# Moving the first head's operand preparation into the projection block of a two-layer encoder step, with key stores ahead of value stores and sink sums by column

## The chip, the cores and the metric

The kernel runs on one core of one Trainium2 chip. The metric is the device time of one execution in microseconds (us), lower is better; for the kernel before, three runs are given by their median. The engines are PE (TensorE, matmul; PEld are its weight loads), DVE (VectorE), ACT (ScalarE), POOL (GpSimd) and SP (SyncE, which here only issues DMAs and waits).

## The reference

One inference step of an encoder trunk of two layers over 1024 prompt rows and 32 sample rows, model width 1024, all in float32. Each layer projects the normalised rows to queries, keys, values and forget gates, runs three groups of attention heads of width 64, normalises each group, projects back, and runs a squared-ReLU MLP; each half ends in a residual sum and a layer norm. The three groups differ in their reach and bias:

```
A: 6 heads, 2 key/value heads   own chunk of 64 + 2 before, T5 bias, a learned sink per head
B: 5 heads                      own chunk + 8 before, clipped relative bias
C: 5 heads                      causal over all rows, logit += sum of log forget gates
...
s = q . k * d ** -0.5 + bias
m = max(max_s(s), sink)                                   (A; the others have no sink)
p = exp(s - m);  p = p / (sum_s(p) + exp(sink - m))
o = p . v
```

The new keys and values of the prompt and of the sample are outputs as well, as are the logs of the forget gates.

## The kernel before, in words

**Blocks.** The program is a sequence of blocks, per layer: the in-projection, prompt attention, sample attention, out-projection, MLP. In a block every engine has its own list of instructions, executed in order, and the engines wait for each other by semaphores written out by hand. A block ends in a barrier of all engines, so the next one begins when the last engine is through.

**In-projection (from line 986).** The weights come as ten chunks, `IN_CH`: three of keys (0 to 2), three of values (3 to 5), four of queries (6 to 9). Each is loaded by SP into one of two buffers `w_raw`, split into a high and a low part (ACT writes the high part, `high_part`, L1162; POOL subtracts, `low_parts`, L1058, and then frees the buffer through `raw_free`), and used by PE in three passes (L378, L1117). Keys and queries are projected transposed into `qk_t`, read by DVE (L1207, L1209); values go row-wise into `v_rows` (L1245). During the value chunks PE turns the keys of each tile of 128 rows back (`turn_k`, L1095, two halves per tile), DVE copies them into the one buffer `k_stage` (L1253), and SP stores them to the outputs (`store_k`, L1007). DVE may write the next tile's keys only when the stores of the tile before have landed (L1250). Between these, DVE works off ten condition tiles (`conditions`, L292): each is a 128x1024 tile of adaLN weights, loaded by SP (`sp_conditions`, L283) into one buffer as soon as DVE has released it. In SP's list the load of the last of these tiles (number 9) stands ahead of the weights of chunk 7, of the value stores and of the last three key stores (L1040 to L1046). At the end DVE reads query tile 7, finishes the cumulated gates, and SP stores them for use as the bias of the C heads.

**Prompt attention (from line 1328).** The 16 heads are worked off in the order A, B, C, each in eight items: one item is 128 query rows, from the last to the first. Per item PE computes the scores from stacked operands (`scores`, L1440: keys in a high and a low part, each twice, over 128 partitions; queries stacked as high and low part), DVE adds the bias and takes the row maximum (`logits`, L1564), ACT takes the exponential and its row sum (L1506), PE turns the probabilities (L1456), ACT and DVE split them into two parts (L1519, L1572), PE multiplies by the values (L1472), and DVE adds the two halves (`head_out`, L1582). After a head's last item DVE forms the inverse of the row sums (L1593); for an A head it first adds the exponentials of the sinks, one operation on 128x8 (L1589). POOL prepares the operands ahead: key parts for each new key head (L1390 to L1395), query parts (L1402, L1404), the mask in the corners of the bias tile (L1408, L1409), value parts (L1416, L1418), and it scales the finished heads (L1381). Keys, queries, bias and values have two buffers each, by the number of the head.

**The start of prompt attention.** For the first head ACT copies the first key head into both halves of `keys_hi` (L1492) after it has loaded its tables, DVE subtracts (L1536), then makes `minus_sink` (L1538), the rounded identity (L1540) and the rounded causal mask (L1541, `causal_r`). POOL makes the first queries and, when SP's bias DMA (L1346) has landed, the masks. PE waits for the rounded constants, the keys and the queries:

```
                    pe.wait_ge(d_rounded, 2)
                    scores(0)
```

`raw` (the two `w_raw` buffers) lies at the start of the work area, `w_hi` and `w_lo` after it. In attention the queries and biases of both buffers lie where `w_raw` was, the key parts where `w_hi` was.

Of the kernel before, what the change touches and what calls it, by code (L numbers as in the profile page):

```python
# [17 lines left out]
F32 = mybir.dt.float32  # L18
# [5 lines left out]
P = 128  # L24
# [42 lines left out]
def build(nc, io):  # L67
# [28 lines left out]
    with ExitStack() as ctx:  # L96
# [96 lines left out]
        ks_hi = [at(f"keys_hi{s}", D0 + 4096 * s, [P, SEQ], F32R) for s in range(2)]  # L193
        ks_lo = [at(f"keys_lo{s}", D0 + 8192 + 4096 * s, [P, SEQ], F32R) for s in range(2)]
# [3 lines left out]
        q_st = [at(f"queries{s}", W0 + 4096 * s, [P, SEQ], F32R) for s in range(2)]  # L198
        bias_h = [at(f"bias{s}", W0 + 8192 + 4096 * s, [P, SEQ]) for s in range(2)]
# [365 lines left out]
        GROUPS = ((0, 384), (384, 320), (704, 320))  # L565

# [357 lines left out]
        for l in range(DEPTH):  # L924
# [60 lines left out]

            with nc.Block() as block:
                @block.sync
                def _(sp):
# [51 lines left out]
                    sp_conditions(sp, "B", l, 9, 10)  # L1040
                    sp_weights(sp, l, 7, 1)
                    for t in range(NTT):
                        sp.wait_ge(b_ev, V_EV - NTT + t + 1)
                        store("v", t, v_tok[:, t, :], b_vout)
                        if t % 3 == 2:
                            store_k(6 + t // 3)  # L1046
                    sp_weights(sp, l, 8, 2)
                    sp.wait_ge(b_rows, 3)
# [4 lines left out]
                def _(pool):  # L1053
# [24 lines left out]
                    for n in range(2, IN_CH):  # L1078
                        low_parts(n)
                        if n < 8:  # L1080
                            products(done, done + (4, 4, 3, 4, 4, 1)[n - 2])
                            done += (4, 4, 3, 4, 4, 1)[n - 2]

# [57 lines left out]
                def _(act):  # L1141
# [46 lines left out]
                    high_part(9)  # L1188

                @block.vector  # L1190
                def _(dve):
# [107 lines left out]
                    query(6)  # L1299
                    query(7)  # L1300
# [14 lines left out]
            span = {"a": 2, "b": 5, "c": NPT}  # L1315
# [12 lines left out]
            with nc.Block() as block:  # L1328
                @block.sync
                def _(sp):  # L1330
                    def bias(hn):
                        g, h = heads[hn][0:2]
                        if hn >= 2:
                            sp.wait_ge(d_lg, NPT * (hn - 1))
                        if g == "a":
                            dst, src = bias_h[hn % 2][:, 0:2 * P], bass.AP(scr_a.tensor, h * P * EXT_A + 127,
                                                                           [[EXT_A - 1, P], [1, 2 * P]])
                        elif g == "b":
                            dst, src = bias_h[hn % 2][:, 0:5 * P], bass.AP(scr_b.tensor, (l * BH + h) * (P * EXT_B) + 127,
                                                                           [[EXT_B - 1, P], [1, 5 * P]])  # L1340
                        else:
                            if h == 0:
                                sp.wait_ge(b_fout, 32)
                            dst, src = bias_h[hn % 2][:].rearrange("p (i t) -> p i t", t=P), \
                                bass.AP(scr_f.tensor, h * P, [[0, P], [CH * P, NPT], [1, P]])
                        sp.dma_start(dst, src).then_inc(d_bias[hn % 2], 16)  # L1346

                    sp.wait_ge(b_bias, 16 * (BH + (AH if l == 0 else 0)))
                    bias(0)
# [19 lines left out]
                def _(pool):  # L1369
# [13 lines left out]
                    for hn, (g, h, qt, half, kt, vc, oc) in enumerate(heads):  # L1383
# [16 lines left out]
                        q = qk[a:a + 64, qt, 0:SEQ]  # L1400
                        hi = q_st[s][a:a + 64, :]
                        own.did(pool.tensor_copy(hi, q))  # L1402
                        own.settle()
                        own.did(pool.tensor_tensor(q_st[s][64 - a:128 - a, :], q, hi.bitcast(F32), ALU.subtract), d_qb)  # L1404
                        if g != "c":
                            w = span[g] * P
                            pool.wait_ge(d_bias[s], 16 * (hn // 2 + 1))
                            own.did(pool.memset(bias_h[s][0:64, w - 64:w], -MASKED), d_mask)  # L1408
                            own.did(pool.memset(bias_h[s][64:P, 0:64], -MASKED), d_mask)  # L1409
                        if first_of[m] == hn:  # L1410
# [4 lines left out]
                            own.settle()  # L1415
# [10 lines left out]
                def _(pe):  # L1426
                    def scores(n):
# [3 lines left out]
                        if i == NPT - 1:  # L1431
                            pe.wait_ge(*((d_kb, m) if m else (d_first, 2)))
                            pe.wait_ge(d_qb, hn + 1)
                        if n >= 2:
                            pe.wait_ge(d_lg, n - 1)
# [40 lines left out]
                    pe.wait_ge(d_rounded, 2)  # L1476
# [10 lines left out]
                def _(act):  # L1487
                    load_tables(act)
                    first = heads[0]
                    a0 = 64 * first[3]  # L1490
                    for a in (a0, 64 - a0):
                        act.activation(ks_hi[0][a:a + 64, :], qk[a0:a0 + 64, Q_TILES + first[4], 0:SEQ], ACT.Copy)\  # L1492
                            .then_inc(d_first_hi, 1)
# [36 lines left out]
                def _(dve):  # L1530
                    own = Own(dve, dve_step)
                    first = heads[0]
                    a0 = 64 * first[3]
                    for i, a in enumerate((a0, 64 - a0)):
                        dve.wait_ge(d_first_hi, i + 1)
                        dve.tensor_tensor(ks_lo[0][a:a + 64, :], qk[a0:a0 + 64, Q_TILES + first[4], 0:SEQ],  # L1536
                                          ks_hi[0][a0:a0 + 64, :].bitcast(F32), ALU.subtract).then_inc(d_first, 1)
# [38 lines left out]
                    def head_out(n):  # L1576
# [7 lines left out]
                        if i == 0:  # L1584
                            c = slice(NPT * (hn % 2), NPT * (hn % 2 + 1))
                            dve.wait_ge(d_ex, n + 1)
                            if heads[hn][0] == "a":
                                dve.wait_ge(d_es, hn + 1)
                                own.did(dve.tensor_tensor(den[:, c], den[:, c], esk[:, c], ALU.add))  # L1589
# [720 lines left out]
```

## Time and profile before

| | us |
|---|---|
| median of three runs | 3181.93 |
| lowest, highest | 3179.59, 3183.39 |
| the profiled execution | 3183.84 |
| span of the profiled execution, first to last instruction | 3182.1 |
| PE busy in the span | 2924.9 (92%) |
| DVE busy | 1581.2 (50%) |
| POOL busy | 1525.1 (48%) |
| ACT busy | 875.0 (27%) |

The span is the stretch the trace covers; what lies around it is 1.7 us. A busy share says how long an engine had an instruction in work, not that it set the end: matmuls overlap, and shares are means over stages with different limits. In the trace each instruction has a start, a duration and, in brackets, the idle time of its engine before it with the event that ended it. The granted clock of PE (PEclk) is given as a share of 2.4 GHz: 1.00 is 2.4 GHz, 0.50 is 1.2 GHz.

### The profile page before, as it was taken

The numbers are of one execution on the slowest core, as the hardware profiler recorded it, in microseconds if no ns is written. First come the engines' busy times: TensorE is split into PE (matmuls) and PEld (weight loads), VectorE is DVE, ScalarE is ACT, GpSimd is POOL, SyncE is SP. The second block draws the span as 40 slices with busy tenths as digits, with TensorE's granted clock in tenths as the row PEclk, the third lists the DMA queues.
The fourth block names the chain that finished last, engine by engine and source line by source line (L and its number), as shares of the span: only waits on it lengthen the run. The fifth ranks groups of instructions, "written<-read, shape, count | busy, mean of one in ns | idle before, by whom it ended". The sixth has DMA issues, their size and how long they took to land. (4 is left out here: it accounts for less than half of the span.)

```text
span 3182.1 us, 46999 instructions
## 1 busy us (share of the span) xinstructions
PE 2924.9 (92%) x18646; PEld 2792.0 (88%) x18646; DVE 1581.2 (50%) x3177; ACT 875.0 (27%) x1710; POOL 1525.1 (48%) x716
## 2 busy tenths in 40 slices
PE   5999899887999999999979998998979999999993
PEld 5999789675999999999979897985859999999993
DVE  6552587556433333333775518775653333333347
ACT  1341476425210010011253307663341010001001
POOL 2693497235333443434339818953334443444334
PEclk5999899988999999999769999997989999999996
DMA  5441211431111111110534502114211111111112
GB/s 227 166 167 60 73 48 44 142 114 58 58 41 53 40 52 40 45 47 26 208 142 145 175 14 87 53 45 148 108 55 54 40 53 40 53 40 50 42 47 89
DMA packets 117352, 253.63 MB, mean 80 GB/s; under 512 B 42564, under 2 KB 78952, under 8 KB 103700
## 3 DMA queue, kind: packets, MB, share of 16 engines
q1 hardware_dynamic: 110868, 228.58, 21.0%
q10 hardware_dynamic: 6336, 23.07, 2.1%
q8 instruction: 94, 1.54, 0.2%
q14 instruction: 54, 0.44, 0.0%
HBM read 217.19 MB, written 42.19 MB: 82 GB/s over the span
## 5 line engine op out<-in xcount | busy, mean ns | idle before, releaser
L378 PE MATMUL psum<-u_hi,w_hi 128*128 128x352 f32 x2016 | 650.8, 323 | 3.8 <-DVE v_rows L1245 3.8
L378 PE MATMUL psum<-u_lo,w_hi 128*128 128x352 f32 x2016 | 651.7, 323 | 0.0
L378 PE MATMUL psum<-u_hi,w_lo 128*128 128x352 f32 x2016 | 650.9, 323 | 0.0
L2177 DVE SCALAR_TENSOR_TENSOR acc_t<-psum,mods,acc_t 128x704 f32<-128x704 f32 x720 | 376.2, 578 | 275.0 <-PE psum L378 275.0
L378 PE MATMUL psum<-h_hi,w_lo 128*128 128x352 f32 x1536 | 495.3, 322 | 0.0
L378 PE MATMUL psum<-h_lo,w_hi 128*128 128x352 f32 x1536 | 495.0, 322 | 0.0
L378 PE MATMUL psum<-h_hi,w_hi 128*128 128x352 f32 x1536 | 494.3, 322 | 0.0
L357 POOL CAST w_hi<-w_raw 128x2048 fp32r<-128x2048 f32 x72 | 136.4, 1894 | 638.5 <-DVEq L2170 357.3
L2160 DVE TENSOR_TENSOR h_relu<-h_relu 128x1056 f32<-128x1056 f32 x64 | 112.2, 1754 | 634.2 <-ACT h_relu L2150 634.2
L378 PEld LDWEIGHTS psum<-u_hi,w_hi 128*128 128x128 f32 x2016 | 379.3, 188 | 5.1 <-issue 4.8
L378 PEld LDWEIGHTS psum<-u_lo,w_hi 128*128 128x128 f32 x2016 | 379.6, 188 | 0.0
L378 PEld LDWEIGHTS psum<-u_hi,w_lo 128*128 128x128 f32 x2016 | 379.1, 188 | 0.0
L2150 ACT ACTIVATE h_relu<-psum 128x1056 f32<-128x1056 f32 x64 | 67.4, 1054 | 1102.3 <-PE psum L378 1094.7
L359 POOL TENSOR_TENSOR w_lo<-w_raw,w_hi 128x2048 fp32r<-128x2048 f32 x72 | 359.2, 4989 | 5.8
L1072 POOL TENSOR_TENSOR ada_products<-w_ada_b,c_rows 128x1024 f32<-128x1024 f32 x88 | 239.1, 2750 | 128.7 <-DVE u_lo L499 96.9
L2097 POOL TENSOR_TENSOR h_lo<-h_relu,h_hi 128x1056 fp32r<-128x1056 f32 x64 | 158.2, 2472 | 284.0 <-ACT h_hi L2152 274.4
L378 PEld LDWEIGHTS psum<-h_hi,w_hi 128*128 128x128 f32 x1536 | 289.4, 188 | 0.0
L378 PEld LDWEIGHTS psum<-h_lo,w_hi 128*128 128x128 f32 x1536 | 289.1, 188 | 0.0
L378 PEld LDWEIGHTS psum<-h_hi,w_lo 128*128 128x128 f32 x1536 | 288.5, 188 | 0.0
L1472 PE MATMUL psum<-v_parts,probs_hi 128*128 128x128 f32 x840 | 199.0, 272 | 8.1 <-DVE o_head L1582 5.7
L1472 PE MATMUL psum<-v_parts,probs_lo 128*128 128x128 f32 x840 | 203.6, 278 | 0.0
L1572 DVE TENSOR_TENSOR probs_lo<-psum,probs_hi 128x512 fp32r<-128x512 f32 (+1 forms) x336 | 157.4, 488 | 90.3 <-ACT probs_hi L1519 85.7
(270 smaller groups left out, 5572.0 us busy)
## 6 DMA issues: line engine op xcount, KB each, us to landing
w_raw<-in_w_all SPq DMA_DIRECT2D x86, 1024.0 KB, 4.8
w_ada_b<-in_w_ada_t ACTq DMA_DIRECT2D x44, 512.0 KB, 3.5
w_ada_v<-in_w_ada_t SPq DMA_DIRECT2D x20, 512.0 KB, 3.3
row_tiles<-in_x_prompt SPq DMA_DIRECT2D x16, 512.0 KB, 12.9
scr_o<-o_head SPq DMA_DIRECT2D x32, 256.0 KB, 2.7
row_tiles<-scr_o SPq DMA_DIRECT2D x16, 512.0 KB, 8.9
x_between_norms<-row_tiles SPq DMA_DIRECT2D x16, 512.0 KB, 2.6
mlp_rows<-x_between_norms SPq DMA_DIRECT2D x16, 512.0 KB, 7.2
```

What stands on the lines that cost most here:

```text
L357: pool.tensor_copy(hi[:, 0:c], raw[s][:, 0:c]).then_inc(pool_step, 1)
L359: pool.tensor_tensor(lo[:, 0:c], raw[s][:, 0:c], hi[:, 0:c].bitcast(F32), ALU.subtract).then_inc(pool_step, 1)
L378: mm = pe.matmul(out[:, b, :], w[s][:, c:c + P], a[:, k, b * NB:(b + 1) * NB], start=(k == 0 and w is w_hi and a is a_hi), stop=(k == n - ...
L1072: pool.tensor_tensor(ada_prod[c][:], ada_b[i % 2][:], c_rows[:, c, :], ALU.mult).then_inc(b_prod, 1)
L1472: mm = pe.matmul(psum[:, 6 + n % 2, 0:2 * HD], p[n % 2][:, b, :], v, start=(b == 0 and p is pt_hi), stop=(b == nb - 1 and p is pt_lo))
L1572: own.did(dve.tensor_tensor(pt_lo[n % 2][:, c:c + w, :], psum[:, 4 + g % 2, 0:w * P].rearrange("p (b c) -> p b c", c=P), pt_hi[n % 2][:, c ...
L2097: pool.tensor_tensor(h_lo[par][:, m, :], h_r[m][:], h_hi[par][:, m, :].bitcast(F32), ALU.subtract).then_inc(h_rdy, 1)
L2150: act.activation(h_r[m][:].rearrange("p (b c) -> p b c", c=NB), lin[m], ACT.Relu).then_inc(h_ev[m], 1)
L2160: dve.tensor_tensor(h_r[m][:], h_r[m][:], h_r[m][:], ALU.mult).then_inc(h_sqd, 1)
L2177: ins = dve.scalar_tensor_tensor(a, y, mods[:, 40 + m, c:c + 1], a, ALU.mult, ALU.add)
```

## The change

The first head's tiles (buffer 0 of keys, queries and bias) move to the two `w_raw` buffers, each free when its last chunk (8 and 9) is split; buffer 1 moves to where `w_hi` was. With that the first head's preparation is written into the in-projection block: ACT's two key copies behind its last high part, SP's bias DMA behind the last weight load, POOL's masks behind its last low part, and on DVE, between the reads of query tiles 6 and 7, the two key subtractions and the query parts (which POOL made before). PE's wait for the rounded constants moves to the first C head, the first that uses them. In SP's list the key stores come ahead of the value store of the same step, and the load of condition tile 9 goes behind the third value store. The sink sums are made column by column, eight operations on 128x1 in place of one on 128x8, with the second summand as a scalar per partition. POOL's waits in the head loop are rewritten to fit.

```diff
-        ks_hi = [at(f"keys_hi{s}", D0 + 4096 * s, [P, SEQ], F32R) for s in range(2)]
-        ks_lo = [at(f"keys_lo{s}", D0 + 8192 + 4096 * s, [P, SEQ], F32R) for s in range(2)]
+        ks_hi = [at(f"keys_hi{s}", (W0, D0)[s], [P, SEQ], F32R) for s in range(2)]
+        ks_lo = [at(f"keys_lo{s}", (W0, D0)[s] + 4096, [P, SEQ], F32R) for s in range(2)]
...
-        q_st = [at(f"queries{s}", W0 + 4096 * s, [P, SEQ], F32R) for s in range(2)]
-        bias_h = [at(f"bias{s}", W0 + 8192 + 4096 * s, [P, SEQ]) for s in range(2)]
+        q_st = [at(f"queries{s}", (W0 + WB, D0 + 8192)[s], [P, SEQ], F32R) for s in range(2)]
+        bias_h = [at(f"bias{s}", (W0 + WB, D0 + 8192)[s] + 4096, [P, SEQ]) for s in range(2)]
...
+        def mask_bias(pool, hn):
+
+            s, w = hn % 2, span[heads[hn][0]] * P
+            pool.wait_ge(d_bias[s], 16 * (hn // 2 + 1))
+            pool.memset(bias_h[s][0:64, w - 64:w], -MASKED).then_inc(d_mask, 1)
+            pool.memset(bias_h[s][64:P, 0:64], -MASKED).then_inc(d_mask, 1)
...
                     store_k(5)
-                    sp_conditions(sp, "B", l, 9, 10)
                     sp_weights(sp, l, 7, 1)
                     for t in range(NTT):
                         sp.wait_ge(b_ev, V_EV - NTT + t + 1)
-                        store("v", t, v_tok[:, t, :], b_vout)
                         if t % 3 == 2:
                             store_k(6 + t // 3)
+                        store("v", t, v_tok[:, t, :], b_vout)
+                        if t == 2:
+                            sp_conditions(sp, "B", l, 9, 10)
                     sp_weights(sp, l, 8, 2)
+                    sp.wait_ge(b_bias, 16 * (BH + (AH if l == 0 else 0)))
+                    sp.wait_ge(raw_free, IN_CH + 2)
+                    load_bias(sp, l, 0)
                     sp.wait_ge(b_rows, 3)
...
+                    mask_bias(pool, 0)
...
                     high_part(9)
+                    act.wait_ge(b_ev, K_EV)
+                    act.wait_ge(raw_free, IN_CH + 1)
+                    for a in (a_first, 64 - a_first):
+                        act.activation(ks_hi[0][a:a + 64, :], first_keys, ACT.Copy).then_inc(d_first_hi, 1)
...
                     query(6)
+                    for i, a in enumerate((a_first, 64 - a_first)):
+                        dve.wait_ge(d_first_hi, i + 1)
+                        dve.tensor_tensor(ks_lo[0][a:a + 64, :], first_keys, ks_hi[0][a_first:a_first + 64, :].bitcast(F32),
+                                          ALU.subtract).then_inc(d_first, 1)
+                    dve.wait_ge(raw_free, IN_CH + 2)
+                    dve.wait_ge(b_ev, V_EV + 1)
+                    q, hi = qk[a_first:a_first + 64, heads[0][2], 0:SEQ], q_st[0][a_first:a_first + 64, :]
+                    cond.did(dve.tensor_copy(hi, q))
+                    cond.settle()
+                    dve.tensor_tensor(q_st[0][64 - a_first:128 - a_first, :], q, hi.bitcast(F32), ALU.subtract).then_inc(d_qb, 1)
                     query(7)
...
                         if hn >= 2:
                             pool.wait_ge(d_sc, NPT * (hn - 1))
-                        q = qk[a:a + 64, qt, 0:SEQ]
-                        hi = q_st[s][a:a + 64, :]
-                        own.did(pool.tensor_copy(hi, q))
-                        own.settle()
-                        own.did(pool.tensor_tensor(q_st[s][64 - a:128 - a, :], q, hi.bitcast(F32), ALU.subtract), d_qb)
-                        if g != "c":
-                            w = span[g] * P
-                            pool.wait_ge(d_bias[s], 16 * (hn // 2 + 1))
-                            own.did(pool.memset(bias_h[s][0:64, w - 64:w], -MASKED), d_mask)
-                            own.did(pool.memset(bias_h[s][64:P, 0:64], -MASKED), d_mask)
+                        if hn >= 1:
+                            q = qk[a:a + 64, qt, 0:SEQ]
+                            hi = q_st[s][a:a + 64, :]
+                            own.did(pool.tensor_copy(hi, q))
+                            own.settle()
+                            pool.tensor_tensor(q_st[s][64 - a:128 - a, :], q, hi.bitcast(F32), ALU.subtract).then_inc(d_qb, 1)
+                            pool.wait_ge(d_qb, hn + 1)
+                            if g != "c":
+                                mask_bias(pool, hn)
+                                pool.wait_ge(d_mask, 2 * (hn + 1))
...
                             pe.wait_ge(d_qb, hn + 1)
+                            if hn == AH + BH:
+                                pe.wait_ge(d_rounded, 2)
...
-                    pe.wait_ge(d_rounded, 2)
                     scores(0)
...
-                                own.did(dve.tensor_tensor(den[:, c], den[:, c], esk[:, c], ALU.add))
+                                for q in range(NPT * (hn % 2), NPT * (hn % 2 + 1)):
+                                    own.did(dve.tensor_scalar(den[:, q:q + 1], esk[:, q:q + 1], den[:, q:q + 1], None, ALU.add))
                                 own.settle()
```

The bodies that moved (`load_bias` with the sources of the three biases, ACT's and DVE's first-head lines in the attention block) are the same instructions as before.

## Rows read from the trace of the kernel before

**Rows 1.** Waits of PE, layer 1, 60 to 356 us: total, times, longest.

```profile
PE psum L1440 <- DVE causal_r L1541: 11.4, 1, 11.4
PE psum L1095 <- DVE k_stage L1253: 5.7, 1, 5.7
PE psum L378 <- DVE v_rows L1245: 2.0, 1, 2.0
```

**Rows 2.** Waits of PE, layer 2, 1660 to 1920 us.

```profile
PE psum L1095 <- DVE k_stage L1253: 5.0, 1, 5.0
```

**Rows 3.** Timeline at the start of attention, by engine: start, duration, engine, line.

```profile
342.34 1.26 DVE L1209 TENSOR_SCALAR qk_t<-psum 128x1056 f32<-128x1056 f32 x1 [10.74 <-PE psum L378]
...
347.48 3.71 DVE L1536 TENSOR_TENSOR keys_lo<-qk_t,keys_hi 64x1024 fp32r<-64x1024 f32 x2 [3.30 <-ACT keys_hi L1492]
351.22 1.03 DVE L1538 TENSOR_SCALAR minus_sink<-sink 128x6 f32<-128x6 f32 x1
...
354.52 0.48 DVE L1564 CUSTOM_DVE_ANT_0 logits<-psum,bias,minus_sink 128x256 f32<-128x256 f32 x1 [1.04 <-PE psum L1440]
...
345.10 1.28 ACT L235 ACT_TABLE_LOAD   x1 [47.51 <-PEq L986]
...
345.10 1.03 POOL L1402 CAST queries<-qk_t 64x1024 fp32r<-64x1024 f32 x1 [42.79 <-POOLq L986]
...
350.19 2.04 POOL L1418 TENSOR_TENSOR v_parts<-v_rows,v_parts 128x512 fp32r<-128x512 f32 x1
```

**Rows 4.** Timeline of POOL, a later head of layer 1.

```profile
380.36 0.61 POOL L1416 CAST v_parts<-v_rows 128x512 fp32r<-128x512 f32 x1
381.05 1.19 POOL L1418 TENSOR_TENSOR v_parts<-v_rows,v_parts 128x512 fp32r<-128x512 f32 x1
```

**Rows 5.** Timelines of POOL, SP and DVE in the value projection of layer 1.

```profile
220.60 5.58 POOL L1058 TENSOR_TENSOR w_lo<-w_raw,w_hi 128x2048 fp32r<-128x2048 f32 x1
...
227.37 0.34 SPq L283 DMA_DIRECT2D w_ada_v<-in_w_ada_t  x1
...
230.24 0.53 SPq L1005 DMA_DIRECT2D out_p_b_k<-k_stage  x1
...
239.37 0.56 DVE L1253 COPY k_stage<-psum 128x384 f32<-128x384 f32 x1 [11.19 <-DMA out_p_b_k<-k_stage]
...
240.65 1.76 DVE L292 CUSTOM_DVE_ANT_0 ada_products_v<-w_ada_v,c_rows 128x1024 f32<-128x1024 f32 x1
```

**Rows 6.** Busy time by stretch: stretch, length, engines (instructions), PEclk, DMA share, GB/s.

```profile
248.00:250.00 2.00, 2.00 (x8) 2.00 (x8) 0.04 (x1) 0.05 (x1) 0.00 (x0) 0.50 0.72 242
...
390.00:392.00 2.00, 2.00 (x12) 2.00 (x12) 0.89 (x4) 1.25 (x5) 1.57 (x2) 0.50 0.33 76
1812.00:1814.00 2.00, 0.73 (x5) 0.76 (x6) 1.74 (x7) 1.76 (x1) 0.00 (x0) 1.00 0.51 184
```

**Rows 7.** Timeline of DVE, sums with the sinks (line 1589), layers 1 and 2.

```profile
385.36 1.68 DVE L1589 TENSOR_TENSOR denominator<-denominator,exp_sink 128x8 f32<-128x8 f32 x1
...
397.38 0.16 DVE L1589 TENSOR_TENSOR denominator<-denominator,exp_sink 128x8 f32<-128x8 f32 x1
...
1949.97 0.97 DVE L1589 TENSOR_TENSOR denominator<-denominator,exp_sink 128x8 f32<-128x8 f32 x1
...
1959.45 0.15 DVE L1589 TENSOR_TENSOR denominator<-denominator,exp_sink 128x8 f32<-128x8 f32 x1
...
1968.11 0.16 DVE L1589 TENSOR_TENSOR denominator<-denominator,exp_sink 128x8 f32<-128x8 f32 x1
```

**Rows 8.** Timelines of DVE and POOL in a layer norm chain of layer 1.

```profile
725.40 0.15 DVE L755 TENSOR_SCALAR row_figures<-tile_mean_var 128x1 f32<-128x1 f32 x1
725.47 0.14 DVE L776 TENSOR_SCALAR row_figures<-row_figures 128x1 f32<-128x1 f32 x1
...
728.71 0.21 DVE L761 SCALAR_TENSOR_TENSOR row_figures<-row_figures 128x1 f32<-128x1 f32 x1
...
723.70 2.40 POOL L676 TENSOR_TENSOR row_tiles<-row_tiles,ln_gain 128x1024 f32<-128x1024 f32 x1 [2.90 <-ACT row_tiles L702]
```

More of the change, by code:

```diff
@@ L565, in build, with load_bias @@
         GROUPS = ((0, 384), (384, 320), (704, 320))
+        span = {"a": 2, "b": 5, "c": NPT}
+        def load_bias(sp, l, hn):
+            g, h = heads[hn][0:2]
+            if g == "a":
+                dst, src = bias_h[hn % 2][:, 0:2 * P], bass.AP(scr_a.tensor, h * P * EXT_A + 127,
+                                                               [[EXT_A - 1, P], [1, 2 * P]])
+            elif g == "b":
+                dst, src = bias_h[hn % 2][:, 0:5 * P], bass.AP(scr_b.tensor, (l * BH + h) * (P * EXT_B) + 127,
+                                                               [[EXT_B - 1, P], [1, 5 * P]])
+            else:
+                if h == 0:
+                    sp.wait_ge(b_fout, 32)
+                dst, src = bias_h[hn % 2][:].rearrange("p (i t) -> p i t", t=P), \
+                    bass.AP(scr_f.tensor, h * P, [[0, P], [CH * P, NPT], [1, P]])
+            sp.dma_start(dst, src).then_inc(d_bias[hn % 2], 16)
+        def mask_bias(pool, hn):
[3 more added lines that the diff above has]
+            pool.memset(bias_h[s][64:P, 0:64], -MASKED).then_inc(d_mask, 1)
         NORM_DVE, NORM_ACT, NORM_POOL = (0, 3, 5, 8), (1, 4, 6), (2, 7)
@@ L984, in build @@
             stored_k = stored_v = stores_to(NTT)
+            a_first = 64 * heads[0][3]
+            first_keys = qk[a_first:a_first + 64, Q_TILES + heads[0][4], 0:SEQ]
             with nc.Block() as block:
@@ L1314, in build @@
             first_of = {m: min(n for n in range(NH) if key_head[n] == m) for m in range(NK)}
-            span = {"a": 2, "b": 5, "c": NPT}
             items = [(hn, i) for hn in range(NH) for i in reversed(range(NPT))]
@@ L1331, in bias @@
                     def bias(hn):
-                        g, h = heads[hn][0:2]
                         if hn >= 2:
                             sp.wait_ge(d_lg, NPT * (hn - 1))
[L1335 to L1349, printed above, removed]
+                        load_bias(sp, l, hn)
                     bias(1)
@@ L1414, in _ @@
                                 pool.wait_ge(d_pv, NPT * (last_of[m - 2] + 1))
-                            own.settle()
                             own.did(pool.tensor_copy(hi, v))
@@ L1488, in _ @@
                     load_tables(act)
[L1489 to L1493, printed above, removed]
                     act.activation(q_smp[:], qk[:, 0:Q_TILES, SEQ:T], ACT.Copy)
@@ L1531, in _ @@
                     own = Own(dve, dve_step)
[L1532 to L1537, printed above, removed]
                     own.did(dve.tensor_scalar(minus_sink[:], sink[:], -1.0, None, ALU.mult))
```

## The prediction, made before the change was timed

> **What bounds the kernel now.** I read the views from coarse to fine. The busy shares and the 40 slices of the page come first: the matmul engine (PE) is busy nearly throughout, so only places where PE stands still can be gained. The list of waits of PE, taken over one layer's projection and the start of its attention, then names these places [rows 1]. Apart from the start of the program there are three: 11.4 us before the first score matmul, until DVE has made `causal_r`; 5.7 us in the V projection, where PE may not turn the next keys because DVE has not emptied the bank; and 2.0 us right after it, before the first query projection. Layer 2 repeats the pattern; its key bank costs 5.0 us [rows 2]. Timelines by engine show what fills the first wait [rows 3, 4], the timelines of SP, POOL and DVE what fills the second [rows 5], windows the granted clock [rows 6], and the rows of line 1589 what the sink sums cost [rows 7, 8].
>
> **Step 1, the start of attention.** The block's first instructions run at 345.10, and the first logits at 354.52 [rows 3]. Between them DVE waits for ACT's key copies, subtracts twice (3.71 us from 347.48), and makes `minus_sink`, `ident_r` and `causal_r`; POOL makes the first queries, masks and value parts. The change takes keys, queries and mask out of this stretch and lets PE start without `causal_r`. What is left ahead of the first logits is the three constants on DVE, in its own order. They meet POOL's value parts: `minus_sink`, 128x6, took 1.03 us from 351.22, until POOL's subtraction of 2.04 us from 350.19 was over [rows 3]. So the constants should again end when POOL's pair ends. That pair now comes first: 0.61 + 1.19 us where nothing disturbs it, start to end 1.88 us [rows 4], so it ends at 346.98, and logits begin at about 347.2, 7.3 us earlier. Two layers: 14.6 us. Ends: if the pair is stretched as before (2.04 for 1.19, the cast likewise 1.05), logits start at 348.4, 6.1 earlier; if DVE is through before POOL takes anything, only PE's first scores stand ahead, 1.04 us [rows 3], so 346.1, 8.4 earlier. Hence 12.2 to 16.8 for both.
>
> The moved work is costed at nothing, and this covers it. POOL had been idle 42.79 us before its first instruction of the block [rows 3], and ACT waits through the same end of the projection: the two copies and masks fit. DVE gets its four instructions between the last two query reads: 3.71 for two subtractions, a query cast no longer than one of these subtractions (half of 3.71), one more subtraction, at most 7.4 us in an idle stretch of 10.74 [rows 3]. If that cover were gone, each microsecond over would push the last query read, and with it the barrier, by one. SP issues one more DMA there, behind the weight loads and ahead of the gate stores, which wait for DVE behind the last query read. Attention's own queue gets shorter by it. POOL's new waits for its queries and masks stand where it waited for the operation before, so they add nothing; PE's wait for the constants, now ahead of the first C head, is met long before; the tiles' new places add no wait.
>
> **Step 2, the key stores.** SP stood at the load of condition tile 9, which waits for DVE's work on tile 8, until 227.37; then came that load, the weights, three value stores and only then the key stores, whose second was issued at 230.24. DVE could not reuse `k_stage` until 239.37, 9.1 us after that issue [rows 5]. With the new order SP waits only for POOL's split, which ends at 226.18 [rows 5]. The weights, two value stores and the first key store take what they took (some 2 us), so the second key store goes at 228.2, 2.05 us earlier, with 0.67 of the 2.4 MB ahead of it (by the tiles' sizes) gone. Had it the same 9.1 us to land, DVE would start at 237.3; in proportion to the bytes, at 234.7. Either way something else is late next: DVE needs condition tile 9 itself 1.28 us later (240.65 against 239.37), and that load is now issued at about 229.3 instead of 227.37, behind the stores. With 9.1 us to land as well it is there at 238.4, 2.25 us before 240.65. I take 2.25 per layer at the first query projection. PE's idle time does not vanish but moves from the key bank to the wait for the last value rows (now 2.0 [rows 1]), perhaps 6 us in one piece. The granted clock was 0.50 (1.2 GHz) after that place in layer 1 and 1.00 in layer 2 [rows 6]; after a longer wait I expect 0.50 in both, and three microseconds at half speed cost 1.5. So 2.25 in layer 1, 0.75 in layer 2, 3 us in all. Ends: the tile lands after 240.65 and the clock falls as well, 3 us lost; it lands in time and DVE starts at 234.7, 4.6 per layer, 9 us gained.
>
> **Step 3, the sums with the sinks.** Twelve sums of 128x8 become 96 of 128x1. No row shows a 128x1 sum with a scalar per partition. The nearest: 128x1 with constants took 0.14 to 0.15 us, and the next began 0.07 later; a three-operand form with such a scalar took 0.21 [rows 8]. I take 0.20 for one and 0.12 from start to start: eight cost 7 x 0.12 + 0.20 = 1.04 against 0.16, so 0.88 more per head. Ends: a pitch of 0.07 gives 0.48, no overlap at all (8 x 0.20) gives 1.44. Does a delay of DVE here reach the end? A sum of 0.97 us was followed by 9.48 us to the next sum, one of 0.15 by 8.66: 0.82 longer, the whole delay [rows 7]. So it counts in full, 12 x 0.88 = 10.6.
>
> Against that stands what the old form lost. Three of the twelve sums were long, the two longest shown: 1.68 and 0.97 [rows 7]. They took in two SBUF inputs while POOL worked. A 128x1 operation with one input ran in 0.14 us in the middle of a POOL product of 2.40 us [rows 8], so the new form should not wait. The 1.68 cost far more than itself: 12.02 us to the next sum instead of 8.66, with the clock at 0.50 in between [rows 6, 7]. Removed: 3.36 + 0.82 + about 0.77 for the third, 4.95 in all. Net 10.6 - 4.95 = 5.6 us slower, ends 0.8 (5.8 - 4.95) and 14.2 (12 x 1.44, less the bare waits of 3.1).
>
> The Trainium skill (SBUF — State Buffer, "Who interferes with whom") counts `tensor_scalar` among the operations that can take the port pair shared with POOL, as a sum of two SBUF tensors does. Were that so for these columns, the waits would stay, and step 3 would cost 10.6 instead of 5.6, giving 3174.9; the 0.14 us row speaks against it.
>
> **The sum.** -14.6 - 3.0 + 5.6 = -12.0. The profiled execution took 3183.84 us (span 3182.1), 1.9 above the median of the three runs, 3181.93; taken from the median, 3169.9. A measurement of this kernel can tell about 0.2%, 6.4 us, from no change.
>
> **Rivals.**
> (a) The sums eat the gain: no overlap (14.2), constants held by a stretched POOL pair (-12.2), stores worth 3: -1, so 3181. For it: DVE is the engine that passes delays on. Against: the 0.07 us pitch. Chance 0.16.
> (b) Slower: each delayed sum starves PE long enough for the clock to fall, as after the 1.68 sum, where 3.36 us went and the clock stood at 0.50 [rows 6, 7]. Place: every A head's last tile. If all twelve cost 3.36: 40.3 - 4.95 = 35.4, less 17.6 gained: 18 slower, 3200. It decides where eight columns hold DVE some 1.5 us over; the 0.97 sum did not bring it about. Chance 0.06.
> (c) The start does not move: DVE's moved work does not fit ahead of the last query read, or the barrier comes later by what was taken off. Then only steps 2 and 3 remain, +2.6: 3184.5. Against: 7.4 in 10.74 us. Chance 0.06.
> (d) Everything goes well: constants ahead of POOL (-16.8), stores 9, sums 0.8: 3157. Chance 0.14.
> My forecast, start 12 to 17 us, the other two steps about cancelling: 0.58.
>
> **The numbers.** The forecast alone, by the inner bounds of its terms, reaches from 3163 to 3176. The range takes in most of (d) and the middle of (a): 3160 to 3179. Faster by over 0.2% (below 3175.6): most of the forecast and (d), 0.73. Within 0.2%: (a), (c) and the forecast's edge, 0.19. Slower: (b) and a poor (c), 0.08.
>
> **What would show it.** Step 1: first score matmul within 0.5 us of the block's first instructions, first logits at 2 to 3 us, ended by POOL's value subtraction; DVE's last query read still without delay. Step 2: the second key store issued some 2 us earlier, the wait of PE for `k_stage` below 3 us, and a longer one for `v_rows`; a wait of DVE for tile 9. Step 3: eight columns per head at 0.12 us start to start, none above 0.3, and head intervals of 9.3 to 9.5 us instead of 8.66. The prediction is wrong if the first logits still start more than 4 us after the block, or if head intervals pass 10 us.

## The result: faster by 0.9%, more than twice the forecast

The changed kernel took 3151.43 us (median; 3149.56 to 3154.82), the kernel before, run beside it, 3181.35: a ratio of 0.9911, 95% interval 0.9899 to 0.9923. That is 29.9 us gained where 12 were forecast; the range, from 3160, did not hold it. The profiled execution took 3151.65 us with a span of 3149.8.

The waits of PE over layer 1's projection and the start of its attention (60 to 420 us: total, times, longest), answering to [rows 1]:

```profile
PE psum L1472 <- DVE neg_max L1584: 4.8, 6, 1.6
PE psum L1472 <- PEq L1014: 3.1, 1, 3.1
...
PE psum L378 <- DVE v_rows L1282: 0.4, 1, 0.4
```

All three waits of [rows 1] are gone or nearly so: `causal_r` (11.4) is replaced by 3.1 us of PE's own sequencer at the block's border and at most 1.6 us in one piece for logits (this window reaches further into attention than that of [rows 1]), `k_stage` (5.7) stands in no row any more, and `v_rows` fell from 2.0 to 0.4. The forecast had the key bank's wait move into that last one; it did not.

The timelines of DVE, PE and POOL at the end of the projection and the start of attention, answering to [rows 3]:

```profile
319.95 2.46 DVE L1339 TENSOR_TENSOR keys_lo<-qk_t,keys_hi 64x1024 fp32r<-64x1024 f32 x2
322.44 0.68 DVE L1344 CAST queries<-qk_t 64x1024 fp32r<-64x1024 f32 x1
323.16 1.22 DVE L1346 TENSOR_TENSOR queries<-qk_t,queries 64x1024 fp32r<-64x1024 f32 x1
330.77 1.26 DVE L1246 TENSOR_SCALAR qk_t<-psum 128x1056 f32<-128x1056 f32 x1 [6.39 <-PE psum L378]
...
333.57 0.60 DVE L1558 TENSOR_SCALAR minus_sink<-sink 128x6 f32<-128x6 f32 x1 [0.96 <-PEq L1014]
...
334.35 1.21 DVE L1561 TENSOR_SCALAR causal_r<-causal 128x128 fp32r<-128x128 f32 x1
335.48 0.47 DVE L1584 CUSTOM_DVE_ANT_0 logits<-psum,bias,minus_sink 128x256 f32<-128x256 f32 x1
...
333.72 0.36 PE L1472 MATMUL psum<-keys_hi,queries 128*128 128x256 f32 x1 [3.10 <-PEq L1014]
...
333.54 0.61 POOL L1446 CAST v_parts<-v_rows 128x512 fp32r<-128x512 f32 x1 [39.94 <-POOLq L1014]
...
334.23 1.25 POOL L1448 TENSOR_TENSOR v_parts<-v_rows,v_parts 128x512 fp32r<-128x512 f32 x1
```

DVE's moved work is over at 324.4, and the last query read still waits 6.39 us for PE: its cover held. The block starts at 333.54 and the first logits come 1.94 us later (9.42 before), set by `causal_r`, which ends with POOL's subtraction.

The timelines of SP and DVE in the value projection, answering to [rows 5]:

```profile
211.01 0.45 SPq L343 DMA_DIRECT2D w_raw<-in_w_all  x1
...
219.73 0.50 SPq L1033 DMA_DIRECT2D out_p_b_k<-k_stage  x1
...
226.58 0.34 SPq L283 DMA_DIRECT2D w_ada_v<-in_w_ada_t  x1
...
227.31 0.55 DVE L1290 COPY k_stage<-psum 128x384 f32<-128x384 f32 x1
...
230.46 1.71 DVE L292 CUSTOM_DVE_ANT_0 ada_products_v<-w_ada_v,c_rows 128x1024 f32<-128x1024 f32 x1 [1.80 <-DMA w_ada_v<-in_w_ada_t]
```

The second key store is issued at 219.73, not at 230.24, and the weights at 211.01, ahead of it. DVE's next copy into `k_stage` waits for nothing and comes 12.06 us earlier than the one of [rows 5]. The wait for condition tile 9 that was forecast is there (1.80) and costs PE at most the 0.4 us at `v_rows`.

Busy time by stretch behind the value projection, layer 1 and layer 2, answering to [rows 6] (stretch, length, PE busy with its instructions, PEclk, DMA share, GB/s):

```profile
246.00:250.00 4.00, 4.00 (x27) 1.00 0.27 107
1789.00:1793.00 4.00, 4.00 (x27) 1.00 0.53 143
```

The sums with the sinks (line 1610), two neighbours of layer 1 and the sixth, answering to [rows 7]:

```profile
377.50 1.05 DVE L1610 TENSOR_SCALAR denominator<-exp_sink,denominator 128x1 f32<-128x1 f32 x8
...
387.06 1.06 DVE L1610 TENSOR_SCALAR denominator<-exp_sink,denominator 128x1 f32<-128x1 f32 x8
...
399.36 1.05 DVE L1610 TENSOR_SCALAR denominator<-exp_sink,denominator 128x1 f32<-128x1 f32 x8
```

Eight columns take 1.05 or 1.06 us, in all twelve heads, and the first five heads of a layer are 9.56 us apart, where 8.66 was the undisturbed interval before.

The first score matmul of layer 1 starts 19.8 us earlier (333.72 against 353.54), that of layer 2 35.8 us earlier (1881.95 against 1917.72), which holds what layer 1 had gained as well. So each layer brings some 18 us ahead of its first score. Step 1 explains 8.3 of them at the first score (0.18 us after the block's start instead of 8.44) and 7.5 at the first logits. The rest had to be the stores, or something that the parts do together.

### The profile page after: what moved, and what is told of

The parts are those of the page before. It is cut to its first block and busy times, and to the rows that moved or that the text cites. A ratio compares the mean times of both kernels' runs of the same rounds, so it can differ in the third digit from the quotient of the medians.

```text
span 3149.8 us, 47125 instructions
## 1 busy us (share of the span) xinstructions
PE 2912.8 (92%) x18646; PEld 2779.7 (88%) x18646; DVE 1591.6 (51%) x3265; ACT 874.9 (28%) x1710; POOL 1517.1 (48%) x712
```

## The experiments

All times are compared with the kernel before, run on the same chip beside them (3179.69 to 3181.21 us); where two of these runs are set against each other, it is by these distances.

**The stores.** Theory T was that the load of condition tile 9 had held SP and all that stood behind it. Rival O was that the order in the queue counts, rival R that the stores were worth 3 us and the first head's move the rest.

`stores_old`: after, with SP's list as before.

```diff
                     store_k(5)
+                    sp_conditions(sp, "B", l, 9, 10)
                     sp_weights(sp, l, 7, 1)
                     for t in range(NTT):
                         sp.wait_ge(b_ev, V_EV - NTT + t + 1)
+                        store("v", t, v_tok[:, t, :], b_vout)
                         if t % 3 == 2:
                             store_k(6 + t // 3)
-                        store("v", t, v_tok[:, t, :], b_vout)
-                        if t == 2:
-                            sp_conditions(sp, "B", l, 9, 10)
```

> The kernel after with SP's order of stores and of the condition tile 9 load as before. Theory T (SP stood at the load of condition tile 9 and everything behind it stood too; two steps, the first head's move and the stores, add up): the store part of about 20 us is lost, 3171 us, the wait of PE for k_stage is back at 5 to 6 us per layer, the second key store is issued near 230 us. Rival R (the stores are worth the 3 us that were predicted, and the rest of the gain comes from the moved first head): 3154 us, PE's wait for k_stage stays near 0.

Measured: 3167.94 us, 0.9966 [0.9955, 0.9977], 11.8 us below before and some 18 above the changed kernel. PE's wait for the key bank is back:

```profile
PE psum L1127 <- DVE k_stage L1289: 5.6, 1, 5.6
```

`stores_only`: before, with the reverse edit.

> The kernel before with the new order of SP alone (key stores first, condition tile 9 behind them); first head and sums as before. Theory T: about 20 us faster than before, 3161 us, second key store issued near 219.5 us, no wait of PE for k_stage, first query projection near 237.5 us. Rival R: 3 us faster, 3178 us, second key store near 228 us.

Measured: 3157.94 us, 0.9939 [0.9922, 0.9955], 21.8 us faster. No row of `k_stage` among PE's waits; first score 343.23 instead of 353.54. Rival R is out: the stores alone are the larger part of the gain.

`tile9_only`: before, with only the tile's load moved.

```diff
                     store_k(5)
-                    sp_conditions(sp, "B", l, 9, 10)
                     sp_weights(sp, l, 7, 1)
...
                         if t % 3 == 2:
                             store_k(6 + t // 3)
+                        if t == 2:
+                            sp_conditions(sp, "B", l, 9, 10)
```

> The kernel before with one edit: the load of condition tile 9 is issued behind the key store that follows the third value store; value stores stay ahead of key stores. Theory T (the waiting load held SP): nearly all of the 20 us, 3161 to 3164 us; the key store is issued about 2 us later than with key stores first, but still near 220 us. Rival O (what counts is that the key store goes ahead of the value store in the queue, with fewer bytes in front of it): 0 to 3 us, 3178 to 3181 us.

`keys_first_only`: before, with only the order of key and value stores turned round, the tile's load where it was.

> The kernel before with one edit: each key store is issued ahead of the third value store of its group; condition tile 9 is loaded where it was. Theory T: SP still stands at the tile until 227.4 us, the second key store goes at about 229.9 instead of 230.2 us, so 0 to 2 us faster, 3179 to 3181 us. Rival O (the order in the queue): most of 20 us, 3161 to 3165 us.

Measured: `tile9_only` 3163.07 us, 0.9955 [0.9938, 0.9971]; `keys_first_only` 3178.51 us, 0.9997 [0.9987, 1.0006]. The timelines of SP and DVE, first of `tile9_only`:

```profile
213.72 6.40 SPq L1005 DMA_DIRECT2D out_p_c_v<-v_rows  x3
...
220.64 0.45 SPq L1005 DMA_DIRECT2D out_p_b_k<-k_stage  x1
227.60 0.34 SPq L283 DMA_DIRECT2D w_ada_v<-in_w_ada_t  x1
...
228.33 0.55 DVE L1254 COPY k_stage<-psum 128x384 f32<-128x384 f32 x1
```

and of `keys_first_only`:

```profile
226.83 0.34 SPq L283 DMA_DIRECT2D w_ada_v<-in_w_ada_t  x1
...
229.15 0.46 SPq L1005 DMA_DIRECT2D out_p_b_k<-k_stage  x1
...
238.44 0.56 DVE L1253 COPY k_stage<-psum 128x384 f32<-128x384 f32 x1 [10.79 <-DMA out_p_b_k<-k_stage]
```

In the first, value stores still go ahead of the key store, and yet it leaves at 220.64, since the tile's load is behind it. In the second the key store leads, and yet leaves at 229.15, since the load is ahead of it; DVE waits as before. Theory T holds, and rival O is out as the main cause. Of the 21.8 us the moved load alone brings 16.6. The remaining 5 of `stores_only` over `tile9_only` are not taken apart: the two intervals overlap, and at the first scores `tile9_only` is 0.3 us ahead in layer 1 and 2.8 behind in layer 2.

**The sums and the moved start.** Theory S was step 3, theory D that DVE's delays are absorbed, and C that the moved work gives part of its gain back.

`one_sum`: after, with the old form of the sum.

```diff
-                                for q in range(NPT * (hn % 2), NPT * (hn % 2 + 1)):
-                                    own.did(dve.tensor_scalar(den[:, q:q + 1], esk[:, q:q + 1], den[:, q:q + 1], None, ALU.add))
+                                own.did(dve.tensor_tensor(den[:, c], den[:, c], esk[:, c], ALU.add))
```

> The kernel after with one 128x8 sum of two SBUF tensors per A head as before, instead of eight columns. Theory S (as in step 3: the eight columns cost 0.88 us per head that passes on in full, and the one sum costs only where POOL holds it off): without the columns 10.6 us go, what POOL's waits bring back is up to 8 us, so 2.6 to 10.6 us faster than the kernel after (the step's own net value says 5.6 us: 3146 us); head intervals 8.66 us except behind long sums. Rival D (a delay of DVE is absorbed by the buffers, the columns cost nothing): no faster than the kernel after, 3151 us, intervals of 9.5 us stay.

`columns_only`: before, with the reverse edit.

> The kernel before with the eight columns alone. Theory S: 4 to 6 us slower than before (12 x 0.88 less 4.95 for the three waits that go), 0.1 to 0.2%; the sums at 9.5 us from each other, none long. Rival D: faster, by the waits that go, 3 to 5 us.

`start_only`: after, with the old form of the sum and the stores as in `stores_old`.

> The kernel after with the old order of stores and the one sum: only the first head's parts are moved. Theory (parts add up): 14.6 us less than before, 0.46%, at most some microseconds off by where POOL's waits fall; first logits 2 us after the block's start. Rival C (moving work ahead of the barrier delays the last query read or the barrier, and part of the gain comes back there): 7 to 10 us less; the block then starts later than 345.1 us.

Measured: `one_sum` 3156.68 us, 0.9928 [0.9914, 0.9943]: by the medians 5 us slower than with the columns, which neither theory had. The two intervals overlap, so the 5 us are not clear of noise; its runs lie between 3153.15 and 3167.54, and the profiled one, at 3165.07, is among the longest. `columns_only` 3182.89 us, 1.0006 [0.9997, 1.0014]: not told from no change. `start_only` 3184.05 us, 1.0012 [1.0003, 1.0021]: the move that brings 7 us per layer at the first logits brings nothing at the end. Rival C's sign is not there, for the block of `start_only` starts at 343.2, not later than 345.1. What happened stands at the sums. Timelines of DVE and POOL of `start_only`, at the third and the sixth sum of layer 1, and the clock behind the sixth (columns as above):

```profile
376.13 2.37 POOL L1435 TENSOR_TENSOR queries<-qk_t,queries 64x1024 fp32r<-64x1024 f32 x1
...
376.73 1.79 DVE L1608 TENSOR_TENSOR denominator<-denominator,exp_sink 128x8 f32<-128x8 f32 x1
...
409.72 2.37 POOL L1425 TENSOR_TENSOR keys_lo<-qk_t,keys_hi 64x1024 fp32r<-64x1024 f32 x1
...
409.75 2.37 DVE L1608 TENSOR_TENSOR denominator<-denominator,exp_sink 128x8 f32<-128x8 f32 x1
...
414.00:416.00 2.00, 2.00 (x12) 0.50 0.00 0
...
420.00:424.00 4.00, 4.00 (x19) 0.50 0.58 147
```

and the same place of the kernel before:

```profile
415.58 2.39 POOL L1394 TENSOR_TENSOR keys_lo<-qk_t,keys_hi 64x1024 fp32r<-64x1024 f32 x1
418.05 2.38 POOL L1395 TENSOR_TENSOR keys_lo<-qk_t,keys_hi 64x1024 fp32r<-64x1024 f32 x1
...
418.02 0.16 DVE L1589 TENSOR_TENSOR denominator<-denominator,exp_sink 128x8 f32<-128x8 f32 x1
```

Before, the sixth sum of layer 1 began in the 0.08 us between two subtractions of POOL, by luck, and took 0.16. With the start moved it begins 0.03 us after such a subtraction and is not through until POOL is: 2.37. That happens in both layers (2.36 in layer 2), and a sum of 1.8 us comes at the third head of both. In layer 1 the reciprocal of the seventh head follows 24.55 us after that sixth sum, against 15.17 before: 9.4 lost, 2.2 of them in the sum, the rest at a clock of 0.50. In layer 2 it was 1.9 (17.11 against 15.17). From the first to the seventh reciprocal `start_only` takes 10.0 us longer than before in layer 1 and 3.9 in layer 2, which is 13.9 of the 15.0 that its first logits had gained. In the profile of `one_sum` the sixth sums take 2.35 and 2.34 us, the clock stands at 0.50 behind both, and the seventh head's reciprocal follows after 23.97 and 24.52 us.

`pair_reduce`: after, with denominators and sink terms in one tile and one reduction over pairs, a single input of 128x16.

```diff
-        den = keep("denominator", [P, 2 * NPT])
-        esk = keep("exp_sink", [P, 2 * NPT])
+        den_esk = keep("denominator", [P, 2, 2 * NPT])
+        den, esk = den_esk[:, 0, :], den_esk[:, 1, :]
...
-                                for q in range(NPT * (hn % 2), NPT * (hn % 2 + 1)):
-                                    own.did(dve.tensor_scalar(den[:, q:q + 1], esk[:, q:q + 1], den[:, q:q + 1], None, ALU.add))
+                                pair = den_esk[:].rearrange("p a c -> p c a")[:, c, :]
+                                own.did(dve.tensor_reduce(rden[:, c], pair, AX_X, ALU.add))
...
```

The reduction writes where the reciprocal wrote, so the reciprocal works in place and the wait for the head two before (`d_norm`) moves ahead of the reduction; in the trace DVE waits ahead of none of the twelve.

> The kernel after with the denominators and the sink terms laid side by side in one tile and summed by one reduction over pairs (128x8x2, one SBUF input) instead of eight columns. Theory S with one input (only a sum that takes two SBUF inputs is held off by POOL): about 0.2 us in place of 1.05 per head, never long, 12 x 0.85 = 10 us faster than the kernel after, 3141 us. Rival P (the reduction is held off as the two-input sum was): 3146 us or so, with one to three long ones among twelve.

Measured: 3142.86 us, 0.9882 [0.9868, 0.9896], 38.3 us below before and so 8.4 us below the changed kernel. All twelve reductions take 0.16 us, wherever they fall. Timelines of POOL and DVE at the sixth:

```profile
397.65 2.38 POOL L1426 TENSOR_TENSOR keys_lo<-qk_t,keys_hi 64x1024 fp32r<-64x1024 f32 x1
...
397.70 0.16 DVE L1612 TENSOR_REDUCE inv_denominator<-denominator 128x8 f32<-128x16 f32 x1
```

It begins 0.05 us into the same subtraction that had held the two-input sum for 2.37, and is done in 0.16. So it is the form of the operation that is held, and not its place or the semaphores: the sum of two SBUF tensors is held, the reduction over one is not. The Trainium skill (SBUF — State Buffer, "Who interferes with whom") says that a DVE instruction with two SBUF inputs contends with a POOL instruction that reads SBUF, and that a reduction never contends on trn2; these rows agree with both.

One SBUF input is not enough by itself, though. The constants at the start of attention have one, and they are held. The run `best` below makes two of them away from POOL's subtractions; timeline of DVE:

```profile
320.40 0.16 DVE L1337 TENSOR_SCALAR minus_sink<-sink 128x6 f32<-128x6 f32 x1
...
405.49 0.22 DVE L1619 TENSOR_SCALAR causal_r<-causal 128x128 fp32r<-128x128 f32 x1
```

In the changed kernel they take 0.60 and 1.21 beside POOL. The columns of 128x1 are the same kind of operation and are held in no head, although the sixth eight of layer 1 begin 0.34 us into a subtraction of 2.37. What sets 128x1 apart from 128x6 was not tried.

Two more kernels ask whether the parts add up once the sum can't be held: `pair_only` (before, with this reduction) and `start_pair` (`pair_reduce` with the stores as in `stores_old`).

> The kernel before with the one reduction over pairs alone (first head and stores as before). Theory H (what made the moved start worth nothing without the columns is the two-input sum that falls into POOL's subtractions; with a sum that POOL can't hold off the parts add up): the columns-only time less 12 x 0.86 = 10.3 us, so 8.6 us less than before, 0.9973. Rival (sums cost what they last, not more): 0.1% or less.

> The kernel after with the reduction over pairs and the old order of stores, so the moved first head and the new sum. Theory H: 14.9 us (two layers of 7.47) below pair_only, 23.5 us below before, 0.9926, and about 20 us above pair_reduce. Rival (something else in the moved start gives its gain back): 8 to 10 us below before, no better than pair_only.

Measured: `pair_only` 3173.54 us, 0.9976 [0.9966, 0.9985], 6.8 us faster than before; `start_pair` 3160.29 us, 0.9936 [0.9920, 0.9953], 20.0 us faster. The moved start is then worth 13.3 us, near twice the 7.48 that the first logits come earlier; with the columns it is worth 13.4 (`columns_only` to `stores_old`), with the old sum it cost 2.8. Theory H holds, with somewhat less than it had forecast (8.6 and 23.5 us).

`held_sum`: does a hold of DVE alone bring the clock down, with nothing that waits for POOL?

```diff
-                                own.did(dve.tensor_reduce(rden[:, c], pair, AX_X, ALU.add))
-                                own.settle()
+                                for _ in range(13 if hn == AH - 1 else 1):
+                                    own.did(dve.tensor_reduce(rden[:, c], pair, AX_X, ALU.add))
+                                    own.settle()
```

> The kernel pair_reduce with the reduction of the sixth A head of each layer done 13 times in a row, so that DVE stands for about 2.3 us where the two-input sum stood for 2.36. Theory H with the clock (a hold of DVE of some 2 us starves PE, its clock falls to 0.50 and stays there for some 15 us): up to 9.4 us per layer as in start_only's layer 1, 19 us in both, at least 2 x 2.2 = 4.4 us if the clock stays at 1.00. Rival A (the hold is absorbed by the buffers): no change. Rival N (the long sum was only a sign of POOL's use of the port, and POOL's side slows the rest): 4.4 us at most, clock 1.00.

Measured: 3159.38 us, 0.9936 [0.9920, 0.9953], 20.9 us below before and so 17.4 above `pair_reduce`. Timelines of DVE and PE, and the clock:

```profile
397.16 2.62 DVE L1613 TENSOR_REDUCE inv_denominator<-denominator 128x8 f32<-128x16 f32 x13
...
401.38 0.74 PE L1488 MATMUL psum<-ident,logits 128*128 128x128 f32 x5 [2.22 <-DVE probs_lo L1592]
...
402.00:404.00 2.00, 2.00 (x15) 0.63 0.00 0
...
414.00:418.00 4.00, 4.00 (x17) 0.50 0.00 0
418.00:422.00 4.00, 4.00 (x28) 0.80 0.00 0
```

From the sixth sum to the next head's reciprocal it takes 24.29 us in layer 1 and 23.45 in layer 2, against 15.16 in both of `pair_reduce`: 9.1 and 8.3 us, 17.4 together, for holds of 2.6. Rivals A and N are out. PE waits 2.22 us for `probs_lo`, its clock falls to 0.50 and comes back only some 17 us later (14 in layer 2).

`best`: `pair_reduce`, with the last constants taken out of the start as well.

```diff
                     query(6)
+                    cond.did(dve.tensor_scalar(minus_sink[:], sink[:], -1.0, None, ALU.mult))
+                    cond.settle()
...
-                    own.did(dve.tensor_scalar(minus_sink[:], sink[:], -1.0, None, ALU.mult))
-                    own.settle()
-                    dve.tensor_copy(ident_r[:], ident[:]).then_inc(d_rounded, 1)
-                    dve.tensor_scalar(causal_r[:], causal[:], -1.0, None, ALU.mult).then_inc(d_rounded, 1)
...
                     for k in range(LAST + 4):
+                        if k == NPT * (AH + 1):
+                            dve.tensor_copy(ident_r[:], ident[:]).then_inc(d_rounded, 1)
+                            dve.tensor_scalar(causal_r[:], causal[:], -1.0, None, ALU.mult).then_inc(d_rounded, 1)
```

> The kernel pair_reduce with minus_sink made in the projection block and ident_r and causal_r made just ahead of the first C head, so that nothing of DVE stands ahead of the first logits but PE's first scores. Expected: first logits about 0.6 us earlier per layer (1.3 instead of 1.95 us after the block's start), so 1 to 2 us below pair_reduce, 3141 to 3142 us, hardly to be told from it; a loss would show if the constants' place holds a head up by more than their 0.3 us.

Measured: 3144.65 us, 0.9894 [0.9878, 0.9911], not to be told from `pair_reduce`. The first logits now wait for PE's first scores alone and come 0.83 us after the block's first instruction (333.99, POOL's); the spans of the two profiled executions differ by 0.6 us (3140.4 and 3141.0), so the microsecond per layer is too little to be seen in the runs:

```profile
334.82 0.48 DVE L1582 CUSTOM_DVE_ANT_0 logits<-psum,bias,minus_sink 128x256 f32<-128x256 f32 x1 [1.76 <-PE psum L1474]
```

Neither of the two is shown to be faster; `pair_reduce` is the simpler one.

## Why the forecast had the sign right and the size wrong

One path through the runs takes the change apart without a gap, by differences to before: columns +1.7, then the start -13.4 (to `stores_old`, -11.8), then the stores -18.1 (to the changed kernel, -29.9). The forecast had +5.6, -14.6 and -3.

**Step 1 held.** In layer 1 the first logits come 7.48 us sooner after the block's start (9.42 less 1.94), for 7.3 forecast, by the mechanism named: the constants end with POOL's pair. Where the sum can't be held the start is worth 13.3 to 13.4 us at the end, for 14.6 forecast. The cover for DVE's moved work held too; it took 4.36 us for the 7.4 allowed. What the step did not see is that moving the start shifts every later sum against POOL's work. That this gain arrives rests on step 3.

**Step 2 failed**, and 15 of the 18 us missed are here. The sentence that failed is "With the new order SP waits only for POOL's split, which ends at 226.18". The split of 220.60 is 128x2048, and so is that of a query chunk; the weights that SP loads there wait for an earlier one, a value chunk of 128x2064. POOL's timeline of the kernel before has it:

```profile
194.80 4.65 POOL L1058 TENSOR_TENSOR w_lo<-w_raw,w_hi 128x2064 fp32r<-128x2064 f32 x1
```

That buffer was free at 199.45. The only thing that kept SP until 227.37 was the load of tile 9; with it moved, SP loads the weights at 211.01, while POOL's 128x2048 split has not begun (219.81 in the changed kernel). The key store then waits for nothing but DVE's copy of those keys and leaves 10.5 us earlier, not 2.05. DVE's copy would have come at 228.18 without its wait (239.37 less 11.19 [rows 5]) and now comes at 227.31, so that wait vanishes whole, and the two sentences that followed, on 9.1 us to land and on idle time that moves to `v_rows`, spoke of a state that never came. The clock was mis-told with it. It was expected at 0.50 in both layers and is 1.00 in both. The forecast also took layer 2 before to be free of the fall, from one row at 1812 us; between the two waits the clock stood at 0.50 there as well. Stretches of the kernel before, columns as above:

```profile
240.00:244.00 4.00, 4.00 (x19) 0.50 0.54 191
248.00:252.00 4.00, 4.00 (x18) 0.63 0.50 158
...
1804.00:1808.00 4.00, 2.60 (x13) 0.51 0.92 349
```

That goes with the part of the gain beyond the waits: in layer 1, PE's waits shrink by 7.3 us (5.7 and 2.0 less 0.4), while `stores_only` has its first score 10.3 us earlier. An estimate from the two rows of layer 1, both with PE busy throughout, gives 2.0 and 1.5 us lost to the clock. The range's end for this step, 9 us gained, came from the same reading; rival (d) at 3157 was therefore too slow as well.

**Step 3 held in its size and missed its context.** The eight columns take 1.05 us for 1.04, at 0.90 more per head for 0.88, and none is long. The Trainium skill (SBUF — State Buffer, "Who interferes with whom") lets `tensor_scalar` contend only when its operands meet conditions, which the step had left out. Of the forms here, 128x1 was not held, 128x6 and 128x128 were. That also corrects the step's reason, one input against two: its own [rows 3] had a one-input operation held.

"So it counts in full, 12 x 0.88" was too much as well: the 0.90 stands between the first five heads of a layer, while from the fifth reciprocal to the sixth it is 0.3 (12.30 against 11.97) and from there to the seventh nothing (14.71 against 14.98). The net value against before was 1.7 (interval -1.0 to +4.5) for 5.6: what the old sums lose in the kernel before was put at 4.95, from three long ones; `pair_only` shows 6.8. Set against the reduction, the columns cost 8.4 us, in the kernel before (`columns_only` to `pair_only`) as in the changed one (to `pair_reduce`). But a net value against before is not what the columns do within this change. With the start moved and the stores old they bring 14.6 us (`start_only` +2.8 to `stores_old` -11.8), with both other parts 5.4 (`one_sum` -24.5 to the changed kernel -29.9), which is not clear of noise.

**The rivals.** (a) and (c) had the start's gain eaten, and neither came. That `start_only`, at 3184.05, lies near (c)'s 3184.5 is chance: (c) held the new stores and the columns, `start_only` has neither, and its first logits did move. (b)'s mechanism exists: a held DVE with the fall of the clock behind it costs 8 to 9 us a time (`held_sum`), more than the 3.36 it was priced at. It struck the old form of the sum and not the columns. Its point of decision, "some 1.5 us over", is not contradicted: behind the sums of 1.05 the clock stays at 1.00 in all twelve heads, while behind sums of 1.7 to 1.8 at the third head it fell in both layers of `start_only` and in layer 2 of `one_sum`, but not in layer 1 of `one_sum`.

Open: why the clock fell behind the sixth sum in layer 1 of `start_only` and not in layer 2, although PE's wait for `probs_lo` behind it was as long (1.98 and 1.96 us). In `one_sum` and `held_sum` it fell behind all four.

## What to carry to other kernels

In a queue that works in order, list every instruction that waits, find for each the one release that it waits for (shape and count of the row must fit), and see what stands behind it: one load that waits early holds everything after it, whatever the order of the rest. Two edits of one pipeline need not add up while an operation in it has a time that depends on where it falls against another engine: here the moved start cost 2.8 us with the old sum and brought 13 with either new one. Take such an operation out first (here a sum of two SBUF inputs beside POOL), then measure the rest. And price a hold of an engine that feeds PE with the clock behind it, not by its own length alone.

## What was not expected of the hardware

A two-input sum of 128x8 took 0.16 us or anything up to the 2.37 us of the POOL subtraction that it fell into; some hundredths of a microsecond in its start decided which. One-input operations of 128x6 and 128x128 were held as well (0.60 for 0.16 us, 1.21 for 0.22), columns of 128x1 were not. A hold of DVE of 2.6 us cost 8 to 9 us: behind a wait of PE of 2.22 us its clock stood at 0.50 instead of 1.00 for 14 to 17 us.
